# Layer 1's first four modulation blocks and three fifth blocks: from TensorE products to VectorE sums

## What is computed

```python
def modulation(cvec, w_ada, b_ada):
    return jnp.split(jax.nn.silu(cvec) @ w_ada + b_ada, 3, axis=-1)

for i in range(DEPTH):
    w_ada, b_ada, g_pre, g_post, mixer = layers[i]
    need_ctx = i < DEPTH - 1
    sh_l, sc_l, gt_l = modulation(c, w_ada, b_ada)
    sh_c, sc_c, gt_c = modulation(c_ctx, w_ada, b_ada)
    h_l = rmsnorm(x_lat, g_pre) * (1.0 + sc_l[:, None, :]) + sh_l[:, None, :]
    h_c = rmsnorm(x_ctx, g_pre) * (1.0 + sc_c) + sh_c
    y_l, y_c = mixer(h_l, h_c, need_ctx=need_ctx)
    x_lat = x_lat + gt_l[:, None, :] * rmsnorm(y_l, g_post)
    if need_ctx:
        x_ctx = x_ctx + gt_c * rmsnorm(y_c, g_post)
```

## Time and profile before

| | us |
|---|---|
| median of the runs | 1611.03 (1610.5 to 1612.84) |
| the profiled execution | 1609.28 |
| its span | 1607.5 |
| TensorE busy | 1589.6 |
| VectorE busy | 629.0 |
| GpSimd busy | 503.8 |
| ScalarE busy | 404.1 |

### The profile page before, as it was taken

The page is one execution under the profiler, slowest core; times in us unless marked ns, Lnnn a source line. Parts: engine busy times, 40 slices in busy tenths (PEclk is TensorE's granted clock), DMA queues, the critical chain, the costliest instruction groups (busy, mean ns, idle before and its releaser), DMA issues.

```text
span 1607.5 us, 18879 instructions
## 1 busy us (share of the span) xinstructions
PE 1589.6 (99%) x7227; PEld 1006.5 (63%) x7227; DVE 629.0 (39%) x1557; ACT 404.1 (25%) x1060; POOL 503.8 (31%) x501
## 2 busy tenths in 40 slices
PE   8999999999999999999999999999999999999999
PEld 3875555468456447885474767658745444788853
DVE  2633342334322233773572424245622223222254
ACT  2104453321243221011362215411242320100000
POOL 1525554132163132430260217546522210010051
PEclk9999999999999999999999999999999999999999
DMA  9452230321440313134423431147533223433341
GB/s 363 169 225 104 84 158 1 149 103 65 168 179 21 131 60 151 59 125 143 189 99 121 178 118 67 53 135 188 213 118 149 105 84 126 156 144 143 145 182 68
DMA packets 23177, 210.75 MB, mean 131 GB/s; under 512 B 3160, under 2 KB 7960, under 8 KB 10672
## 3 DMA queue, kind: packets, MB, share of 16 engines
q1 hardware_dynamic: 19440, 195.74, 32.0%
q0 software_dynamic: 3648, 13.79, 3.1%
HBM read 204.75 MB, written 1.49 MB: 128 GB/s over the span
## 4 chain that ended last, share of the span: by engine, by line
PE 96%; DVE 2%; POOL 1%; ACT 1%; DMA 0%; issue 0%; SPq 0%; DVEq 0%; ACTq 0%
PE bank L737 27%; PE bank L1215 14%; PE bank L1571 9%; PE bank L861 5%; PE bank L875 5%; PE bank L1597 4%; PE bank L1510 4%; PE bank L848 3%; PE bank L799 3%; PE bank L1103 3%; PE bank L1093 3%; PE bank L1127 2%; PE bank L750 2%; PE bank L1118 1%; PE bank L1084 1%; PE bank L1180 1%
## 5 line engine op out<-in xcount | busy, mean ns | idle before, releaser
L737 PE MATMUL bank<-ring,arena 128*128 128x512 f32 (+2 forms) x864 | 357.9, 570 | 1.0 <-DVE arena L1657 1.0
L737 PEld LDWEIGHTS bank<-ring,arena 128*128 128x128 f32 x864 | 161.6, 190 | 178.4 <-issue 167.4
L3092 POOL TENSOR_SCALAR arena<-arena,stat 128x512 f32<-128x512 f32 (+1 forms) x128 | 168.0, 1325 | 176.8 <-DVE stat L1803 176.7
L1571 PE MATMUL bank<-arena,ring 128*128 128x256 f32 (+1 forms) x768 | 152.8, 362 | 0.0
L1571 PEld LDWEIGHTS bank<-arena,ring 128*128 128x128 f32 x768 | 136.0, 190 | 17.0 <-issue 0.5
L2672 ACT ACTIVATE arena<-arena,stat 128x513 f32<-128x513 f32 (+3 forms) x128 | 81.3, 636 | 125.9 <-DVE stat L1795 125.8
L1215 PE MATMUL bank<-arena 128*128 128x256 f32 x432 | 96.4, 379 | 0.0
L861 PE MATMUL bank<-arena,ring 128*128 128x512 f32 (+1 forms) x256 | 90.5, 497 | 0.2 <-DVE arena L1779 0.2
L875 PE MATMUL bank<-ring,arena 128*128 128x512 f32 x192 | 89.4, 601 | 1.2 <-ACT arena L2733 1.2
L1215 PEld LDWEIGHTS bank<-arena 128*128 128x128 f32 x432 | 81.9, 190 | 11.9 <-issue 0.8
L1215 PE MATMUL bank<-arena,ring 128*128 128x256 f32 x384 | 85.4, 380 | 0.0
(11 more groups left out here) (362 smaller groups left out, 2272.7 us busy)
## 6 DMA issues: line engine op xcount, KB each, us to landing
ring<-stream SPq DMA_DIRECT2D x87, 2048.0 KB, 8.1
ring<-stream SPq DMA_DIRECT2D x6, 1024.0 KB, 10.0
arena<-arena POOLq DMA_DIRECT2D x50, 64.0 KB, 3.7
gate_rows<-gate_scratch POOLq DMA_DIRECT2D x3, 1024.0 KB, 5.1
masks_sb<-masks POOLq DMA_DIRECT2D x2, 1024.0 KB, 5.1
arena<-g_scratch POOLq DMA_DIRECT2D x1, 2048.0 KB, 9.9
arena<-rev_scratch POOLq DMA_DIRECT2D x8, 256.0 KB, 6.5
ring<-stream SPq DMA_DIRECT2D x1, 1536.0 KB, 6.9
```

The costliest lines, as they stand in the source:

```text
L737: last = mm(dst, a, b, start=(k == 0), stop=(k == len(pairs) - 1))
L1571: last = mm(ps[:, SEQ * part + cols.start:SEQ * part + cols.stop], w[:, a:a + P], hT2[:, k, cols], start=(k == 0), stop=(k == DC - 1))
L3092: nc.gpsimd.tensor_scalar(row, row, stat[:, 3, s:s + 1], None, ALU.mult).then_inc(w_norm, 1)
```

## The change

Two kinds of block leave `modulation_products`. For each of them VectorE sums, over the eight chunks, chunk times condition value (a [128, 512] multiply-add per chunk and condition vector, `add_chunk`), which leaves two totals of [128, 512] for a block; TensorE then only adds the 128 partitions, with products whose 32 stationary columns are zero but for one column of ones (`unit_row`).

The first four blocks of layer 1: `early_sum` does one chunk, so two operations, in each of the steps 1 to 32 of the first attention, ahead of the row maxima of the step. The eight totals lie in XN (the squares of half 0 go to HT instead). `early_modulation` takes them with 16 products behind output tile 2 of half 0, and the turn comes behind tile 3; `scale_columns(1)` moves there too, and ScalarE's wait for it from the first tile to the first of half 1.

The fifth block (ada 4) of layers 1, 2 and 3: `late_sums` does four chunks behind tile 1 and four behind tile 2 of half 0. Behind half 1 `late_modulation` does ada 5's eight products as before and four with the totals.

A ring slot that VectorE has read is released by VectorE's flags. z's groups are spread over steps 0 to 5, 8, 9, 12, 13, 16, 17, 20, 21; the four groups that had to share a bank no longer do. GpSimd clears `unit` at the start with three memsets. In the second block's beside plan, hidT 0 moves from before merge group 2 to behind it. Declarations and call sites that say no more are left out:

```diff
@@ -74,8 +74,7 @@
 
 MODULATION_STEPS = [("ada", _i, 8, _at) for _i, _at in enumerate((0, 1, 3, 7))] + [("turn", 0, 0, 11)]
 LATENT_STEPS = [("ada", _i, 8, _at) for _i, _at in enumerate((0, 1, 2, 8))] + [("turn", 0, 0, 10)]
-BESIDE = {0: [("z", 1, 4, 0), ("z", 2, 4, 2), ("z", 3, 4, 4), ("ada", 0, 8, 6), ("ada", 1, 8, 9), ("z", 4, 4, 10),
-              ("z", 5, 4, 14), ("z", 6, 4, 16), ("ada", 2, 8, 18), ("z", 7, 4, 19), ("ada", 3, 8, 22), ("turn", 0, 0, 24)],
+BESIDE = {0: [("z", 1, 4, 0), ("z", 2, 4, 2), ("z", 3, 4, 4), ("z", 4, 4, 8), ("z", 5, 4, 12), ("z", 6, 4, 16), ("z", 7, 4, 20)],
           1: LATENT_STEPS, 2: MODULATION_STEPS, 3: [("z", _i, 4, 2 * _i - 2) for _i in range(1, 8)]}
 BESIDE_BLOCKS = {0: [("ada", 0), ("ada", 1), ("z", 1), ("ada", 2), ("ada", 3)], 3: [("z", 1)]}
@@ -144,8 +143,8 @@
 def branch_items():
 
     merge = lambda j, a=0, b=DC: [("m", (j, k), 0.87) for k in range(a, b)]
-    items = [("cum", 0, 1.1), ("hid", 0, 1.9), ("cumT", 0, 1.2), ("hid", 1, 1.9), ("hidT", 0, 0.3)] + merge(2)
-    items += [("hidT", 1, 0.3), ("cmp begin", 0, 0.0)] + merge(3, 0, 4) + [("cmp", 0, 1.0)] + merge(3, 4)
+    items = [("cum", 0, 1.1), ("hid", 0, 1.9), ("cumT", 0, 1.2), ("hid", 1, 1.9)] + merge(2)
+    items += [("hidT", 0, 0.0), ("hidT", 1, 0.6), ("cmp begin", 0, 0.0)] + merge(3, 0, 4) + [("cmp", 0, 1.0)] + merge(3, 4)
@@ -211,6 +210,8 @@
             out += [(f"{layer} oT", va(6)), (f"{layer} y0", "vv"), (f"{layer} oT", "va"), (f"{layer} y0", "vv")]
+        elif layer == 0:
+            out += [("0 y0", "vvv"), ("1 early", "v"), ("0 y0", "v"), ("1 turn", "v")]
         else:
             out += [(f"{layer} y0", "v" * q_tiles)]
...
-LATE_BANK, ONE_BANK = 4, [f"0 z{_i}" for _i in range(4, 8)]
+LATE_BANK = 4
...
-        _last = _last if _stage in ONE_BANK else (_last + 1) % 2
+        _last = (_last + 1) % 2
...
+        unit = sbuf("unit", [P, STRIP + 2 * EARLY])
...
+        modulation_sums = [probs[:, r, 0:HALF] for r in range(2)]
+        early_sums = [[XN[:, HALF * (2 * i + r):HALF * (2 * i + r + 1)] for r in range(2)] for i in range(EARLY)]
+        unit_row = lambda m: unit[:, 2 * EARLY - 1 - m:2 * EARLY - 1 - m + STRIP]
+        no_row = unit[:, 2 * EARLY:]
...
-        block_free_at, groups_begun, modulations = {}, [0], []
+        groups_begun, modulations = [0], []
+        block_free_at = {BLOCK_AT[f"{_l} ada 4"]: (flag("late_sums_ready"), _l) for _l in range(1, 4)}
+        block_free_at |= {BLOCK_AT[f"1 ada {_i}"]: (flag("early_sums_ready"), _i + 1) for _i in range(EARLY)}
...
+            def early_modulation():
+
+                ps = begin(modulation_group(1, "early"))
+                pe.wait_ge(flag("unit_ready"), 1)
+                pe.wait_ge(flag("early_sums_ready"), EARLY)
+                for i, sums in enumerate(early_sums):
+                    for half in range(2):
+                        for r in range(2):
+                            strip, cols = slice(STRIP * (2 * half + r), STRIP * (2 * half + r + 1)), slice(SEQ * half, SEQ * half + SEQ)
+                            if i == 0:
+                                last = mm(ps[strip, :], no_row if half else unit_row(r), sums[r], start=True, stop=False,
+                                          tile_position=(0, strip.start))
+                            else:
+                                last = mm(ps[strip, cols], unit_row(2 * i + r), sums[r][:, cols], start=False, stop=(i == EARLY - 1),
+                                          tile_position=(0, strip.start))
+                last.then_inc(made, 1)
+
+            def late_modulation(layer):
+
+                g, w = modulation_group(layer, "late"), weights(f"{layer} ada 5")
+                ps = begin(g)
+                for k in range(DC):
+                    strip = slice(STRIP * (k % 4), STRIP * (k % 4 + 1))
+                    last = mm(ps[strip, :], cond_strip[:, k, 2 * EARLY - 4:2 * EARLY - 4 + STRIP], w[:, k * HALF:(k + 1) * HALF],
+                              start=(k < 4), stop=False, tile_position=(0, strip.start))
+                last.then_inc(modulation_made, 1)
+                modulations.append((layer, 5))
+                block_free_at[BLOCK_AT[f"{layer} ada 5"]] = (modulation_made, len(modulations))
+                pe.wait_ge(flag("unit_ready"), 1)
+                pe.wait_ge(flag("late_sums_ready"), layer)
+                for half in range(2):
+                    for r in range(2):
+                        strip, cols = slice(STRIP * (2 * half + r), STRIP * (2 * half + r + 1)), slice(SEQ * half, SEQ * half + SEQ)
+                        last = mm(ps[strip, cols], unit_row(r), modulation_sums[r][:, cols],
+                                  start=False, stop=True, tile_position=(0, strip.start))
+                last.then_inc(made, 1)
...
@@ -1268,11 +1313,15 @@
                         else:
                             project(groups[half * tiles + t],
                                     [(src[:, chunk(k), rows(t)], w[:, k * HALF:(k + 1) * HALF]) for k in range(DC)])
+                        if layer == 0 and half == 0 and t == 2:
+                            early_modulation()
+                        if layer == 0 and half == 0 and t == 3:
+                            modulation_turn(1, "early")
                         if half and t:
                             turn_tile(f"{NEXT[layer]} hT", t - 1, 4 * (layer + 1))
                     weights_done(f"{layer} out{half}")
-                    if layer < 3:
-                        modulation_products(layer + 1, 4 + half)
+                    if layer < 3 and half:
+                        late_modulation(layer + 1)
...
@@ -1817,6 +1866,8 @@
 
                 for i in range(n + QUAD_OUT):
                     beside_step(layer, i)
+                    if layer == 0 and 1 <= i <= EARLY * DC:
+                        early_sum(i - 1)
                     if i < n:
                         row_maximum(i)
...
+            def add_chunk(w, k, totals, done):
+
+                for r in range(2):
+                    chunk, by = w[:, k * HALF:(k + 1) * HALF], cond_strip[:, k, 2 * EARLY - 2 + r:2 * EARLY - 1 + r]
+                    if k == 0:
+                        step(vec_op.tensor_scalar(totals[r], chunk, by, None, ALU.mult))
+                    elif (k, r) == (DC - 1, 1):
+                        settle()
+                        vec_op.scalar_tensor_tensor(totals[r], chunk, by, totals[r], ALU.mult, ALU.add).then_inc(done, 1)
+                    else:
+                        dve.wait_ge(steps, taken[0] - 1)
+                        step(vec_op.scalar_tensor_tensor(totals[r], chunk, by, totals[r], ALU.mult, ALU.add))
+
+            def late_sums(layer, chunks):
+
+                w, arrived, value = ring_block(f"{layer} ada 4")
+                dve.wait_ge(arrived, value)
+                if chunks[0] == 0 and layer == 3:
+                    dve.wait_ge(d_turned, len(decay))
+                for k in chunks:
+                    add_chunk(w, k, modulation_sums, flag("late_sums_ready"))
+
+            def early_sum(at):
+
+                w, arrived, value = ring_block(f"1 ada {at // DC}")
+                dve.wait_ge(arrived, value)
+                add_chunk(w, at % DC, early_sums[at // DC], flag("early_sums_ready"))
...
                     if KINDS[layer] == "mlstm" and t == 2:
                         save_heads(3)
                     gated(t)
+                    if layer == 0 and t > 1:
+                        save_modulation(1, ("early", "turn")[t - 2])
+                        if t == 3:
+                            scale_columns(1)
+                    if layer < 3 and t in (1, 2):
+                        late_sums(layer + 1, range(4 * t - 4, 4 * t))
...
                     mlstm(layer)
-                if layer < 3:
+                if 0 < layer < 3:
                     scale_columns(layer + 1)
                 residual(layer, tiles)
...
             def squares_of_y(layer, tiles):
                 for i, g in enumerate(y_groups(layer)):
                     half, t = i // tiles, i % tiles
-                    if half == 0 and t == 0 and layer < 3:
+                    if (half, t) == (int(layer == 0), 0) and layer < 3:
                         sc.wait_ge(flag("mod_ready"), layer + 1)
...
                     ps = wait_made(g)
-                    act_op(xn[:, t, HALF * half:HALF * (half + 1)], ps[:, :], ACT.Square,
+                    unused = HT[:, HALF * t:HALF * (t + 1)] if (layer, half) == (0, 0) else xn[:, t, HALF * half:HALF * (half + 1)]
+                    act_op(unused, ps[:, :], ACT.Square,
                            accum_out=sq[:, 4 + 2 * t + half:5 + 2 * t + half]).then_inc(flag("y_squared"), 1)
...
             step(nc.gpsimd.memset(probs_t[:, 1, :], 0.0))
             nc.gpsimd.memset(cond_strip[:, :, :], 0.0).then_inc(flag("strip_cleared"), 1)
+            step(nc.gpsimd.memset(unit[:, 0:2 * EARLY - 1], 0.0))
```

(2 more changed lines are left out.)

## The result

The changed kernel takes 1616.11 us (median of 8 runs, 1614.45 to 1621.75). Beside it the kernel before took 1611.03 (1609.33 to 1614.46, 8 runs). The ratio is 1.0038, 95% interval [1.0028, 1.0047]: 5.1 us slower. The forecast was slower by 11.0, a time of 1622.0: the sign is right and the size about twice too large. The profiled execution took 1617.44 (span 1615.6), 8.2 above the one of before (1609.28).

A forecast was written before the change was run, and what follows sets the result against it. TensorE, busy 99% of the span, was taken to bound the kernel. 20.1 us of added waits less 9.1 saved gave +11.0: 1620.3 profiled, 1622.0 with the 1.75 allowance; range from 1604 with 2 for its margin up to 1628.

The forecast's parts named there:

- The sum of work: TensorE sheds 13.0 us of ada blocks and takes on 3.9 of added products: 9.1 saved if no one waits.
- narrow pairs: First attention, context-query steps (256 keys) without z products, such as 14 and 15: each of three pairs 2.2 us late.
- wide pairs: First attention, latent-query steps (512 keys) without z products, 10, 11 and 18, 19: each pair 4.5 us late.
- step 24: First attention, a wide step (512 keys) without z products: 2.0 us late.
- steps 25 to 31: First attention, under 1.82 us of output products a step: 26 late by 1.3, 27 0.4, 28 1.6, others near 0.
- tail: End of the first attention: turn 30 waits for a scaling that the last sums held up, 2.3 us.
- z1's load: 2 MB block issued at the end of step 5's z, needed 8.5 us later at step 8: 0 wait, 0.4 to spare.
- the port: VectorE's sums and GpSimd's scalings share SBUF ports in the attention; a sum meeting a GpSimd operation waits for all of it.
- the walk: Durations laid end to end through the first attention's steps: 23.4 us late in all, 20.1 added to today's.
- sums without the port: Rival: scalings don't shut sums out, a bare step holds only 1.2 us more, 10.4 in all: 1609; chance 0.11.
- its own case: The likeliest case, sums making TensorE wait in the attention: 1622.0, own range 1616 to 1629; chance 0.63.
- Hidden sums: Rival: sums fall into VectorE's idle time only, TensorE keeps 9.1 us less 1.8 at step 8: 1604; chance 0.22.

The follow-up runs named there:

- the port run: Changed kernel, 36 of 64 sum operations reading their addend from an idle PSUM bank instead of SBUF, z's groups sharing the other bank: 1616.79 us.
- reciprocals first: Changed kernel, in layer 0 the reciprocals of step i-1 put ahead of row maximum i, behind the sums: 1611.66 us.
- sums behind: Changed kernel, `early_sum` moved from ahead of the row maximum to the end of the iteration, one chunk an iteration: 1614.78 us.
- sums behind in the cover: Changed kernel, `early_sum` at the iteration's end, two chunks where the own step issues z products, one in 24 to 31: 1613.46 us.
- sums in the covered steps, ahead of the row maximum: Changed kernel, two chunks in each iteration following a z step, one in 26 to 31, none in other iterations up to 25: 1622.4 us.

## Why the prediction was right, and where it was not

**The sum of work** (9.1 saved) held in each term that the runs show: the fifth blocks alone are 3.2 to 4.8 faster for a forecast of 4.1, the early products take 2.3 for 2.4, and VectorE's busy time in the attention rose by 40 us (58.8 to 99.2) for 39.

**The waits** were 16.8 for a forecast of 20.1, by these terms (forecast, then the trace): narrow pairs 3 x 2.2, 3 x 1.9; wide pairs 2 x 4.5, 2 x 3.9; step 24 2.0, 1.2; steps 25 to 31 3.3, 0.34; tail 2.3, 2.2; z1's load 0, 0.6; clock 0, 2.8 in the z groups. From each sum the 3.3 of today's waits go off, which leaves 17.3 by the trace's terms, near the 16.8. Most wrongly sized were the steps under output products, and the clock, which the forecast did not have at all and which took about 5 us, those inside the wide pairs counted.

**The step that failed is the port.** "Waits for the whole of it" did not happen to VectorE: the sum that began 0.14 behind a scaling took 1.09, where by the walk it would have had to wait some 1.4 first, and no sum took over 1.18. It had been read from rows against GpSimd's tensor_tensor and carried over to a tensor_scalar; the row of 791.79 that seemed to confirm it showed only GpSimd's side, and that side came true ("some 512-wide scalings at 1.9 to 2.0": three took 1.99, and two 2.57). The rule in the Trainium skill, SBUF — State Buffer, "Who interferes with whom", that whoever comes second is blocked for the whole instruction, isn't what VectorE's 1.09 shows either. (The 0.32 by which the prediction had GpSimd's tensor_tensor grow compares two operations with different inputs, 646.88 and 649.31 in the earlier trace rows, and shows no growth by itself.) By the walk the two sums of a wide pair's second step need 3.95 us, from 9.65 to 13.6; in the trace they took 1.75 (173.03). And the port run leaves TensorE's idle time where it was.

What stood in its place is the queue. The walk made the *scores* late by row maxima ("scores 8, 12, 16, 20, 24 the late ones"); the trace has the *turns* late (8.7 us, the scores 0.2), by reciprocals that stand behind sums and row maximum. The rival "sums without the port" (1609), whose condition was half true, falls too: it counted 1.2 us a bare step, and left out that GpSimd starts a pair late, has no slack in it (10.66 busy without a gap) and that TensorE, having waited, goes on at the lower clock.

**The sign is in part luck.** Without the port the forecast's own terms give 1609, on the faster side. It came out slower because the scalings were late behind the queue and the clock fell; in the walk the price of the port, most of which did not come due, filled the place of both. The lower end of its own case is 1616 ("if the second sum always follows the first at once, and the output-product steps absorb theirs"). It is near the 1616.11 measured, and both of its conditions nearly hold; but it has no clock in it, so that the number fits so well is luck too.

**Hidden sums** fell, though its own condition came nearly true: the row maxima that it named were ready when TensorE came with the next scores (0.2 us of waiting in all). They were not the point that decides. And with 48 of the 64 sums left out the kernel only reached 1607.8, not 1604, as the cover it counted on was needed by today's chain as well. z1's 1.8 at step 8 was right (1.9 without sums).

**From profiled sum to time.** 1620.3 was forecast and 1617.44 measured for the profiled executions, 2.9 off. The medians moved by 5.1 only, since the runs of the changed kernel spread with the clock: 1614.45 to 1615.1 at a mean clock of 0.999, 1616.1 at 0.998, 1617.44 to 1621.75 at 0.997 and 0.996. The profiled run of the changed kernel was one of its slower ones, so the allowance of +1.75 on top of the profiled run went the wrong way.

## What to carry to other kernels

An engine that is 40% busy isn't free: before work is put into its queue, ask which of its results the bound engine waits for next and what stands ahead of that result in the queue; here the order of reciprocals, row maximum and sums was worth 4.5 us (3.1 with the clock's cost taken out), and what the operations read no more than about 1 in the half of it that was tested. Work that TensorE sheds may have been the cover of another chain: price a version with the work removed and next to nothing added first, since here that alone had used up the gain. Compare versions by TensorE's idle time and granted clock, and not by the time alone: here one edit won 2.7 us with more waiting than before it, in a profile whose clock never fell. And split a change whose parts don't need each other: the fifth blocks won 3.2 and the first four lost 8.3.

## What the runs showed of the hardware

- **VectorE and GpSimd on SBUF.** A scalar_tensor_tensor with both tensors in SBUF against GpSimd's tensor_scalar: VectorE's takes 744 ns with GpSimd idle, 1.09 us when it begins 0.14 inside a scaling, 1.18 at most; GpSimd's takes up to 2.57 for 1.57, on average 1680 for 1565 and 1032 for 925; with the addend of most sums in PSUM the 512-wide are at 1588. Against GpSimd's tensor_tensor the same kind of VectorE's took 2.41 and 2.84.
- **The granted clock falls in the midst of dense work.** TensorE was busy 98% of the span, and short waits one behind another cost a half z group 0.55 to 2.2 us. But the same waits don't always do it. z4's half group at step 8, in the changed kernel, with reciprocals first, with sums behind, and with sums behind in the cover:

```profile
158.60 3.67 PE L906 MATMUL bank<-arena,ring 128*128 128x512 f32 x8 [0.63 <-DMA ring<-stream]
```

```profile
158.46 5.37 PE L906 MATMUL bank<-arena,ring 128*128 128x512 f32 x8 [0.70 <-DMA ring<-stream]
```

```profile
161.85 5.25 PE L906 MATMUL bank<-arena,ring 128*128 128x512 f32 x8 [0.95 <-DMA ring<-stream]
```

```profile
158.84 3.67 PE L908 MATMUL bank<-arena,ring 128*128 128x512 f32 x8 [1.07 <-DMA ring<-stream]
```

The longest single wait left the clock at 1.00; the other two had scores waiting 0.81 and 1.10 just before. Which waits bring it down stays open.
- **A load with 0.4 us to spare isn't hidden**: a 2 MB block lands in 7.9 us at the median of all 87, but z1's was issued at 149.88 in the changed kernel and TensorE got on at 158.60, 8.7 later. TensorE waited for it 0.6 to 1.9 in all kernels without the early blocks on TensorE but one, whose TensorE was late itself (sums in the covered steps, ahead of the row maximum).
